# One 512-column product in place of two 256-column ones, with the sum of both halves moved to VectorE

## The chip, the cores and the metric
The kernel runs on one core of one Trainium2 chip. The metric is the device time of one launch in microseconds (us). Three runs of the kernel before gave 2631.38, 2632.57 and 2633.56 us; the median is 2632.57 us.

## The reference, cut to what matters
The reference computes two transformer blocks over 256 tokens (272 with 16 meta tokens in the first), with a model width of 2048, all in float32. Nearly all arithmetic is in dense products of an activation matrix with a weight matrix:

```python
# block 1 (272 tokens; the feed-forward part needs 258, then 256 of them)
proj = rmsnorm(h) @ w_in ; attention of two kinds ; h = h + mix @ w_out
g = x @ w_gate; u = x @ w_up                       # 2048 x 5632 each
h = h + (silu(conv3(g) + conv_b) * u) @ w_down     # 5632 x 2048
# block 2 (256 tokens)
proj = rms_norm(h) @ w_in                          # q, k, v, pool input, gates
m = sigmoid(g0)*(ya @ w_br_a) + sigmoid(g1)*(yb @ w_br_b) + sigmoid(g2)*(yc @ w_br_c)
h = h + m @ w_out
h = h + (silu(h' @ w_gate) * (h' @ w_up)) @ w_down # h' = rms_norm(h)
return rms_norm(h)
```

## The kernel before, in words
**Products.** A float32 product is made of three fp32r products. A weight w is split into its rounded value `whi` and the rest `wlo`, an activation x likewise into `xh` and `xl`, and whi·xh + whi·xl + wlo·xh is added up in PSUM. Weights are the stationary operand, 128x128; the activations (features on partitions, tokens along the free dimension) are the moving one. The moving columns are read alternately from the two halves of the token range (`in_turn`), and who reads PSUM undoes that order (`bank`, `halves`).

**Chunks and groups.** The weights come as a stream of 924 chunks of 128x1024 float32 (512 KB). A chunk holds two row tiles (k) of four output blocks (`ob`) of 128 columns, so that one chunk is 8 pairs of (k tile, block) and 24 matmuls (`chunk`, L1372 to L1374). A group is the run of chunks that fills the four PSUM banks `acc[:, 0..3]`: 8 chunks (CD) for an inner width of 2048, 22 (CF) for 5632, 4 (CH) for 1024. Block `ob` accumulates in bank `ob`, columns 0 to n.

**The pipeline of a chunk.** SyncE loads it to `raw` (a ring of 4 slots). ScalarE (ACT) rounds it to `whi` (`high_part`, L480). VectorE (DVE) subtracts to get `wlo` (`low_part`, L841). TensorE (PE) waits for `lo_ready` at each chunk, and raises `chunk_used` at its end; ACT waits for that of four chunks earlier before it writes a slot. ACT and DVE each run through their instructions in program order and are AHEAD = 2 chunks in front: before they turn to the results of a group, they have made the first two chunks of the next group, and not its third.

**The end of a group.** DVE waits for each block (`wait_block`) and takes it out of PSUM, one 128x256 instruction a block, which raises `bank_free`: times 1/rms into `quad_a`, `quad_b` or `qkvu` (`times_rms`, L861); for the up projection times the activated gate (L1220); for a residual straight into h (L882). PE starts block `ob` of the next group when bank `ob` is free.

**Stages, in order** (chunks): the first block's projections and attention (106, tokens 272 or 258), FFN (11 turns of a gate group of 258 columns and an up group of 256), DOWN (4 groups of 22), IN2 (6 groups), IN2S (8 groups, MOBA attention beside them), MERGEA (4 turns of a gate group and a branch group of 4 chunks, the stick-breaking attention beside them), POOL (2), MERGE (8 turns of gate group and branch group), OUT2 (4 groups), FFN2 (11 turns of gate and up group), DOWN2 (4 groups of 22).

**What follows a group, by stage.** After a gate group of FFN2, ACT applies SiLU (L708), and only then makes `whi` of the up group's third chunk. After an up group (FFN, FFN2), ACT rounds the product to `acth` (L711), DVE subtracts to `actl` (L1224), and only then makes `wlo` of the next group's third chunk. After a gate group of MERGEA and MERGE, ACT applies the sigmoid (L750). After a group of DOWN or OUT2, DVE makes `wlo` of the third chunk, then four parts of `xl` (L891) for which ACT makes `xh` (L502), then waits for ACT's square (L506) and adds it up (L866, L868), and then makes `wlo` of the fourth.

Of the kernel before, what the change touches and what calls it, by code (L numbers as in the profile page):

```python
# [108 lines left out]
def build(nc, hT, wts, vecs, ident, ones, tril, triu, cos_sin, na_bias, relT, onehot,  # L109
# [3 lines left out]
    with ExitStack() as ctx:  # L113
# [8 lines left out]
        xh = sb("xh", [P, DB, L], F32R)  # L122
        xl = sb("xl", [P, DB, L], F32R)
# [74 lines left out]
        acth = at("acth", 0, [P, FFB, SEQ], F32R)  # L198
        actl = at("actl", FFB * SEQ * 4, [P, FFB, SEQ], F32R)

        qkvu = at("qkvu", 0, [P, 56, SEQ])
        yah = at("yah", 57344, [P, HEADS, SEQ], F32R)
        yal = at("yal", 65536, [P, HEADS, SEQ], F32R)
# [14 lines left out]
        ych = at("ych", 24576, [P, HEADS, SEQ], F32R)  # L218
        ycl = at("ycl", 32768, [P, HEADS, SEQ], F32R)
        ybh = at("ybh", 40960, [P, HEADS, SEQ], F32R)  # L220
        ybl = at("ybl", 49152, [P, HEADS, SEQ], F32R)
        msum = at("msum", T0, [P, DB, SEQ])
        mh = at("mh", 0, [P, DB, SEQ], F32R)
        ml = at("ml", T0, [P, DB, SEQ], F32R)
# [12 lines left out]
        bank_free = sem("bank_free")  # L237

# [79 lines left out]
        AT_END = AT_DOWN2.past(4 * CF, 4)  # L318
        assert nc.sbuf_base <= arena
# [31 lines left out]
        def bank(ob, n, rows=slice(0, P)):  # L351

            return acc[rows, ob, 0:n].rearrange("p (a s) -> p s a", s=2)
# [52 lines left out]
        def _(pool):  # L406
# [34 lines left out]
            pool.wait_ge(bank_free, 4 + 4 * AT_MERGEA.g)  # L441
# [31 lines left out]
        def _(act):  # L473
# [19 lines left out]
            def residual(at, b0, gain, cols, dst_cols, chunks, first=0, ahead=False):  # L493

                high_parts(at, chunks, first)
                if ahead:
                    high_part(shifted(at, chunks, 1), 0)
                for ob in range(4):

                    act.wait_ge(bank_free, groups_behind(at, 4, 4 + ob + 1))  # L500
# [202 lines left out]
            def ffn(start, turn0, k, before_silu):  # L703
                def turn(at, i, first):
# [5 lines left out]
                    act.wait_ge(bank_free, groups_behind(at, 4, 4 + 8))  # L710
# [6 lines left out]
            ffn(AT_FFN, 0, 4, 3)  # L717
            high_part(AT_DOWN, 0)
            with act.Fori(0, 2) as i:
                for k in range(2):  # L720
                    residual(shifted(Turn(AT_DOWN, i, 2 * CF, 2), k * CF, k), i * 8 + 4 * k, "mix2_g", slice(META, L),
                             slice(0, SEQ), CF, 1, True)
# [6 lines left out]
            act.wait_ge(bank_free, 4 + 4 * AT_IN2S.g)  # L729
# [18 lines left out]
            def gate(at):  # L748
                act.wait_ge(bank_free, groups_behind(at, 4, 4 + 4))
# [7 lines left out]
            with act.Fori(0, 4) as i:  # L757
                at = Turn(AT_MERGEA, i, CD + CH, 2)
                for j in range(CD + CH):
# [22 lines left out]
                    if j == CD - 1:  # L782
                        gate(at)
# [18 lines left out]
            for i in range(4):  # L802
                for b in range(2):
                    at = AT_MERGE.past((2 * i + b) * (CD + CH), 2 * (2 * i + b))
                    high_parts(at, CD, 1 - b)
                    gate(at)
# [4 lines left out]
            with act.Fori(0, 4) as i:  # L811
                residual(Turn(AT_OUT2, i, CD, 1), i * 4, "ffn2_g", slice(META, L), slice(0, SEQ), CD, 1, True)
            act.preload_act_table_set(LN_EXP)
            ffn(AT_FFN2, 11, 6, 0)
# [5 lines left out]
            for k in range(3):  # L820
                residual(AT_DOWN2.past(k * CF, k), 4 * k, None, slice(META, L), None, CF, min(k, 1), True)
# [15 lines left out]
        def _(dve):  # L837
# [25 lines left out]

            def add_squares(n):
# [5 lines left out]
            def residual(at, b0, chunks, gain, cols, dst_cols, xh0, sq0, scale=None, first=0, ahead=False):  # L870
# [3 lines left out]
                for ob in range(4):  # L874
                    wait_block(at, chunks, ob)
                    src = bank(ob, n)
                    if scale is not None:
                        dve.tensor_tensor(halves(quad_a[:, ob, 0:n]), src, halves(scale[:, 0:n]), ALU.mult)
                        dve.drain()
                        src = halves(quad_a[:, ob, 0:n])  # L880
                    hb = halves(flat(h[:, bass.ds(b0 + ob, 1), cols]))
                    dve.tensor_tensor(hb, src, hb, ALU.add).then_inc(bank_free, 1)  # L882
# [299 lines left out]
            def ffn(start, turn0, k, conv):  # L1182
# [3 lines left out]
                def turn(at, i, done=0):  # L1186
                    low_parts(at, CD, done)
                    dve.wait_ge(rs_ready, k)
                    times_rms(at, CD, lambda ob: (quad_a if conv else quad_b)[:, ob, 0:nt], slice(c0, L))
# [28 lines left out]
                    for ob in range(4):  # L1218
# [21 lines left out]
            times_rms(AT_IN2, CD, lambda ob: qkvu[:, ob, :], slice(META, L))  # L1240
            dve.memset(ss[:], 0.0)
            with dve.Fori(1, 6) as i:
                at = Turn(AT_IN2, i, CD, 1)
                low_parts(at, CD)
                times_rms(at, CD, lambda ob: flat(qkvu[:, bass.ds(i * 4 + ob, 1), :]), slice(META, L))
            with dve.Fori(0, HEADS) as i:
# [12 lines left out]
                times_rms(at, CD, lambda ob: flat(qkvu[:, bass.ds(i * 4 + (3 * HEADS + ob), 1), :]), slice(META, L))  # L1259

            def gates(at):
                times_rms(at, CD, lambda ob: quad_a[:, ob, 0:SEQ], slice(META, L))

            def branch(at, i, gate_n, dst):

                dve.wait_ge(gate_out, gate_n)
                for ob in range(4):
                    wait_block(at, CH, ob)
                    dve.tensor_tensor(halves(dst(ob)), bank(ob, SEQ), halves(quad_a[:, ob, 0:SEQ]), ALU.mult).then_inc(bank_free, 1)
# [8 lines left out]
            with dve.Fori(0, 4) as i:  # L1278
                start = Turn(AT_MERGEA, i, CD + CH, 2)
                for j in range(CD + CH):  # L1280
# [3 lines left out]
                    if j == CD + CH - 1:  # L1284
                        masked_exponentials(hd)
                        branch(shifted(start, CD, 1), i, i + 1, lambda ob: flat(msum[:, bass.ds(i * 4 + ob, 1), :]))
# [35 lines left out]
            with dve.Fori(0, 4) as i:  # L1322
                for b in range(2):
# [5 lines left out]
                    branch(at, i, i * 2 + (5 + b), lambda ob: quad_b[:, ob, 0:SEQ])  # L1329
# [24 lines left out]
        def _(pe):  # L1354
            def chunk(at, j, chunks, x_hi, x_lo, n, blocks=4, width=P, row=GC, per_chunk=2, halfway=None):
# [491 lines left out]
```

## Time and profile before

| | |
|---|---|
| median of three runs | 2632.57 us |
| profiled execution | 2633.74 us, its span 2632.1 us |
| PE, PEld busy | 2608.5 us, 2578.4 us (22,866 instructions each) |
| DVE, ACT, POOL busy | 1658.2, 1252.0, 85.8 us |
| granted TensorE clock | 0.999 of full speed |
| DMA | 497.83 MB, mean 189 GB/s |

PE is the matmul pipe and PEld its weight loads. Matmuls overlap each other, so that the durations of one line add up to more than the span; the pace of PE is read from the starts in the timeline. "Idle before" is the time that an engine stood still just before an instruction, with the work that released it.

### The profile page before, as it was taken

To read this page: it belongs to the slowest core of one execution; us is meant where nothing else is said; L and a number is where in the kernel's file an instruction comes from. 1 tells how busy PE (TensorE), PEld (TensorE's weight loads), DVE (VectorE), ACT (ScalarE), POOL (GpSimd) and SP (SyncE) were. 2 spreads that over 40 slices of the span, in tenths; PEclk is the share of its full clock that TensorE was granted. 3 is DMA by queue.
4 is the path that set the end of the run, shared out by engine and by line. 5 is a ranking of instruction groups with operands and counts; after the bars stand their busy time and mean duration, and the time that the engine had idled before them with its cause. 6 is when DMAs were issued, how large, how long until landed. Compare 5 with 4: busy or idle time off the path is not lost.

```text
span 2632.1 us, 58075 instructions
## 1 busy us (share of the span) xinstructions
PE 2608.5 (99%) x22866; PEld 2578.4 (98%) x22866; DVE 1658.2 (63%) x2223; ACT 1252.0 (48%) x1563; POOL 85.8 (3%) x123
## 2 busy tenths in 40 slices
PE   9999999999999999999999999999999999999998
PEld 8999999999999999999999999999999999999998
DVE  7778786666666555555556776656665555655554
ACT  6456654434444444434445564444554444444443
POOL 0000000000000000000111500000000000000000
PEclk9999999999999999999999999999999999999999
DMA  7543446555565566666555455556555555566655
GB/s 251 156 140 120 150 168 200 192 199 199 183 209 185 205 190 207 199 193 193 190 191 174 160 183 195 200 196 199 194 198 194 197 194 191 191 193 207 199 192 185
DMA packets 138876, 497.83 MB, mean 189 GB/s; under 512 B 16544, under 2 KB 17056, under 8 KB 138752
## 3 DMA queue, kind: packets, MB, share of 16 engines
q1 hardware_dynamic: 135728, 491.34, 56.0%
q0 software_dynamic: 3024, 4.66, 0.9%
q8 instruction: 99, 1.62, 0.2%
q14 instruction: 25, 0.20, 0.0%
HBM read 493.31 MB, written 2.62 MB: 188 GB/s over the span
## 4 chain that ended last, share of the span: by engine, by line
PE 92%; DVE 4%; ACT 2%; DMA 1%; issue 1%; DVEq 1%; SPq 0%; ACTq 0%
PE acc L1372 30%; PE acc L1373 29%; PE acc L1374 29%; DVE wlo L841 1%; PE aux L1425 1%; DMA h<-in_hT 1%; ACT whi L480 1%; PE aux L1405 0%; PE aux L1503 0%; DMA raw<-in_wts 0%; DVEq L914 0%; PE aux L1416 0%; PE aux L1506 0%; PE aux L1619 0%; DVE qn_na L987 0%
## 5 line engine op out<-in xcount | busy, mean ns | idle before, releaser
L841 DVE TENSOR_TENSOR wlo<-raw,whi 128x1024 fp32r<-128x1024 f32 x926 | 1120.6, 1228 | 706.7 <-ACT whi L480 703.2
L1372 PE MATMUL acc<-xh,whi 128*128 128x256 f32 (+3 forms) x4968 | 1377.2, 277 | 4.3 <-DVE wlo L841 2.0
L1374 PE MATMUL acc<-xh,wlo 128*128 128x256 f32 (+3 forms) x4968 | 1367.4, 275 | 0.0
L1373 PE MATMUL acc<-xl,whi 128*128 128x256 f32 (+3 forms) x4968 | 1367.4, 275 | 0.0
L480 ACT ACTIVATE whi<-raw 128x1024 fp32r<-128x1024 f32 x926 | 958.9, 1054 | 791.6 <-PE acc L1374 774.3
L1372 PEld LDWEIGHTS acc<-xh,whi 128*128 128x128 f32 (+1 forms) x4968 | 951.0, 191 | 11.0 <-issue 5.9
L1373 PEld LDWEIGHTS acc<-xl,whi 128*128 128x128 f32 (+1 forms) x4968 | 951.2, 191 | 0.4
L1374 PEld LDWEIGHTS acc<-xh,wlo 128*128 128x128 f32 (+1 forms) x4968 | 951.2, 191 | 0.0
L1372 PE MATMUL acc<-acth,whi 128*128 128x256 f32 x1408 | 387.3, 275 | 0.0
L1373 PE MATMUL acc<-actl,whi 128*128 128x256 f32 x1408 | 387.2, 275 | 0.0
L1374 PE MATMUL acc<-acth,wlo 128*128 128x256 f32 x1408 | 387.2, 275 | 0.0
L1372 PEld LDWEIGHTS acc<-acth,whi 128*128 128x128 f32 x1408 | 270.3, 192 | 0.2 <-DVE wlo L841 0.2
L1374 PEld LDWEIGHTS acc<-acth,wlo 128*128 128x128 f32 x1408 | 270.3, 192 | 0.0
L1373 PEld LDWEIGHTS acc<-actl,whi 128*128 128x128 f32 x1408 | 270.3, 192 | 0.0
L861 DVE TENSOR_TENSOR quads<-acc,rstd 128x256 f32<-128x256 f32 (+1 forms) x136 | 57.9, 425 | 53.6 <-PE acc L1374 53.1
L708 ACT ACTIVATE quads<-quads 128x1024 f32<-128x1024 f32 x22 | 23.3, 1059 | 108.6 <-DVE quads L1206 57.9
L711 ACT ACTIVATE acth<-quads 128x1024 f32 (+1 forms) x22 | 23.3, 1060 | 106.5 <-DVE quads L1220 106.5
L1372 PE MATMUL acc<-mh,whi 128*128 128x256 f32 x256 | 70.4, 275 | 0.0
L1373 PE MATMUL acc<-ml,whi 128*128 128x256 f32 x256 | 70.4, 275 | 0.0
L1374 PE MATMUL acc<-mh,wlo 128*128 128x256 f32 x256 | 70.4, 275 | 0.0
L434 POOL DMA_DIRECT2D bias<-distances x64 | 32.7, 513 | 1022.8 <-PE acc L1374 780.7
L1372 PEld LDWEIGHTS acc<-mh,whi 128*128 128x128 f32 x256 | 49.2, 192 | 0.0
(303 smaller groups left out, 2259.5 us busy)
## 6 DMA issues: line engine op xcount, KB each, us to landing
raw<-in_wts SPq DMA_DIRECT2D x928, 512.0 KB, 4.2
bias<-distances POOLq DMA_DIRECT2D x64, 32.0 KB, 3.5
bias<-in_na_bias POOLq DMA_DIRECT2D x8, 217.7 KB, 3.4
h<-in_hT SPq DMA_DIRECT2D x3, 544.0 KB, 5.1
out_T<-result SPq DMA_DIRECT2D x3, 384.0 KB, 2.8
h<-in_hT SPq DMA_DIRECT2D x2, 272.0 KB, 4.1
distances<-quads POOLq DMA_DIRECT2D x1, 512.0 KB, 12.5
out_T<-result SPq DMA_DIRECT2D x1, 512.0 KB, 2.7
```

Source lines behind the costliest of these rows:

```text
L434: pool.dma_start(bias2[p:p + COPIES, t, :], bass.AP(dist_dram.tensor, i * (DISTS + 1) + (SEQ - 1 - t * P - p), [[HEADS * (DISTS + 1) - 1, ...
L480: act.activation(whi[:, slot_of(at, j), :], raw[:, slot_of(at, j), :], ACT.Copy).then_inc(hi_ready, 1)
L708: act.activation(quad_b[:, :, 0:SEQ], quad_b[:, :, 0:SEQ], ACT.Silu).then_inc(silu_out, 1)
L711: act.activation(acth[:, bass.ds(i * 4, 4), :], quad_a[:, :, 0:SEQ], ACT.Copy).then_inc(act_hi, 1)
L841: dve.tensor_tensor(wlo[:, slot_of(at, j), :], raw[:, slot_of(at, j), :], whi[:, slot_of(at, j), :].bitcast(F32), ALU.subtract).then_inc(l ...
L861: dve.tensor_tensor(halves(dst(ob)), bank(ob, n), halves(scale[:, cols]), ALU.mult)\
L1372: pe.matmul(dst, hi, x_hi(kt), start=kt == 0, stop=False)
L1373: pe.matmul(dst, hi, x_lo(kt), start=False, stop=False)
L1374: last = pe.matmul(dst, lo, x_hi(kt), start=False, stop=kt == chunks * per_chunk - 1)
L1425: last = pe.matmul(aux[:, 3, q:a.nq], a.vt[0:nk, kt, :], a.pt[0:nk, kt, q:a.nq], start=kt == 0, stop=kt == len(a.kt) - 1)
```

## The change
In every group with 256 tokens, but for the branch products (`yah`, `ybh`, `ych`) and the pooling products, the three products of a pair become two: whi times [xh | xl], 512 columns, into both halves of the bank, and wlo times xh, 256 columns, into the first half. Groups of 272 or 258 tokens keep three products. The high and low parts of an activation move into one tile (`xs`, `acts`, `ms`, ...) so that one access pattern reads both. What PSUM then holds in two halves is added by DVE: `sum_parts` reduces 512 columns to 256 a block, and the factor (1/rms, the activated gate) or the residual is applied by one 128x1024 instruction behind it. Those who waited for the fourth `bank_free` of such a group now wait for `group_out`, raised by that last instruction. The last stage's residual (DOWN2) adds the two halves to h one after the other, a 128x256 instruction each.

```diff
-        xh = sb("xh", [P, DB, L], F32R)
-        xl = sb("xl", [P, DB, L], F32R)
+        xs = sb("xs", [P, 2, DB, L], F32R)
+        xh, xl = xs[:, 0], xs[:, 1]
...
+        def both_parts(ob):
+
+            return acc[:, ob, 0:2 * SEQ].rearrange("p (k a s) -> p s a k", k=2, s=2)
...
+            def sum_parts(at, chunks, dst):
+
+                for ob in range(4):
+                    wait_block(at, chunks, ob)
+                    dve.tensor_reduce(halves(flat(dst[:, ob:ob + 1, :])), both_parts(ob), AX_X, ALU.add)\
+                        .then_inc(bank_free, 1)
+                dve.drain()
+
+            def sums_times_rms(at, chunks, dst):
+
+                sum_parts(at, chunks, dst)
+                dve.tensor_tensor(dst, dst, rstd[:, META:L].unsqueeze(1).to_broadcast([P, 4, SEQ]), ALU.mult)\
+                    .then_inc(group_out, 1)
...
+                elif sq0 is not None:
+                    sum_parts(at, chunks, quad_a[:, :, 0:SEQ])
+                    hq = h[:, bass.ds(b0, 4), cols]
+                    dve.tensor_tensor(hq, hq, quad_a[:, :, 0:SEQ], ALU.add).then_inc(group_out, 1)
+                else:
+                    for ob in range(4):
+                        wait_block(at, chunks, ob)
+                        hb = halves(h[:, b0 + ob, cols])
+                        dve.tensor_tensor(hb, bank(ob, SEQ), hb, ALU.add)
+                        dve.drain()
+                        dve.tensor_tensor(hb, bank(ob, SEQ, first=SEQ), hb, ALU.add).then_inc(bank_free, 1)
...
-                    for ob in range(4):
-                        wait_block(at, CD, ob)
-                        dve.tensor_tensor(halves(quad_a[:, ob, 0:SEQ]), bank(ob, SEQ), halves(quad_b[:, ob, 0:SEQ]),
-                                          ALU.mult)\
-                            .then_inc(bank_free, 1)
+                    product = quad_a[:, :, 0:SEQ]
+                    sum_parts(at, CD, product)
+                    dve.tensor_tensor(product, product, quad_b[:, :, 0:SEQ], ALU.mult).then_inc(group_out, 1)
...
-                    act.wait_ge(bank_free, groups_behind(at, 4, 4 + 8))
+                    act.wait_ge(group_out, wide(i))
...
+            def wide_chunk(at, j, chunks, x, x_hi, halfway=None):
...
+                        def low():
+                            return pe.matmul(acc[:, ob, 0:SEQ], wlo[:, slot, c:c + P], x_hi(kt), start=False, stop=False)
+
+                        def high(first, final):
+                            return pe.matmul(acc[:, ob, 0:2 * SEQ], whi[:, slot, c:c + P], x(kt), start=first, stop=final)
+
+                        if kt < 2 * chunks - 1:
+                            high(kt == 0, False)
+                            last = low()
+                        else:
+                            low()
+                            last = high(False, True)
...
+            def both(t, first=0):
+                cols = slice(first, first + SEQ)
+                return (lambda kt: t[:, :, kt, cols].rearrange("p k (s a) -> p k a s", s=2),
+                        lambda kt: in_turn(t[:, 0, kt, cols]))
```

## Rows read from the trace of the kernel before
**Rows 1.** The page: busy time, share of the span, instructions.
```profile
PE 2608.5 (99%) x22866; PEld 2578.4 (98%) x22866; DVE 1658.2 (63%) x2223; ACT 1252.0 (48%) x1563; POOL 85.8 (3%) x123
```
**Rows 2.** Waits of PE: us in total, times, longest.
```profile
PE acc L1372 <- DVE wlo L841: 2.7, 5, 0.8
```
**Rows 3.** Groups by form, PE: count, busy us, mean ns, idle before.
```profile
L1372 PE MATMUL acc<-xh,whi 128*128 128x256 f32 x3776 | 1042.4, 276 | 1.2 <-DVE wlo L841 1.2
```
**Rows 4.** Timeline of PE, 256 columns, first and 30th: start, duration.
```profile
799.73 0.28 PE L1374 MATMUL acc<-xh,wlo 128*128 128x256 f32 x1
...
802.97 0.28 PE L1373 MATMUL acc<-xl,whi 128*128 128x256 f32 x1
```
**Rows 5.** Timeline of PE: 258 columns (first, 13th) and 272 (first, 15th).
```profile
300.16 0.28 PE L1374 MATMUL acc<-mixbh,wlo 128*128 128x258 f32 x1
...
301.50 0.28 PE L1374 MATMUL acc<-mixbh,wlo 128*128 128x258 f32 x1
...
149.87 0.28 PE L1374 MATMUL acc<-xh,wlo 128*128 128x272 f32 x1
...
151.49 0.28 PE L1373 MATMUL acc<-xl,whi 128*128 128x272 f32 x1
```
**Rows 6.** Timeline of PEld where PE stood still: DOWN2's third chunk.
```profile
2390.08 0.19 PEld L1372 LDWEIGHTS acc<-acth,whi 128*128 128x128 f32 x1 [0.17 <-DVE wlo L841]
2390.18 0.19 PEld L1373 LDWEIGHTS acc<-actl,whi 128*128 128x128 f32 x1
```
**Rows 7.** Timeline of PE: a 384-column fp32r matmul and the next.
```profile
1557.96 0.34 PE L1635 MATMUL aux<-sbsh,tril_r 128*128 128x384 f32 x1
1558.14 0.33 PE L1635 MATMUL aux<-sbsl,tril_r 128*128 128x384 f32 x1
```
**Rows 8.** Groups by form, DVE: takes from PSUM, a reduction, a 128x1024 factor.
```profile
L861 DVE TENSOR_TENSOR quads<-acc,rstd 128x256 f32<-128x256 f32 x92 | 39.1, 425 | 35.1 <-PE acc L1374 34.6
L1215 DVE TENSOR_TENSOR quads<-quads,rstd 128x1024 f32<-128x1024 f32 x22 | 26.8, 1219 | 0.0
L904 DVE TENSOR_REDUCE small<-aux 86x3 f32<-86x816 f32 x8 | 8.0, 1003 | 6.1 <-PE aux L1506 6.1
```
**Rows 9.** Timeline of DVE in FFN2: gate group's end, up group's end.
```profile
2063.17 0.42 DVE L861 TENSOR_TENSOR quads<-acc,rstd 128x256 f32<-128x256 f32 x1 [0.25 <-PE acc L1374]
2065.72 3.50 DVE L841 TENSOR_TENSOR wlo<-raw,whi 128x1024 fp32r<-128x1024 f32 x3 [2.12 <-ACT whi L480]
...
2084.61 0.42 DVE L1220 TENSOR_TENSOR quads<-acc,quads 128x256 f32<-128x256 f32 x1 [0.25 <-PE acc L1374]
2087.54 4.75 DVE L841 TENSOR_TENSOR wlo<-raw,whi 128x1024 fp32r<-128x1024 f32 x4
```
**Rows 10.** Timeline of PE: first matmul of third, third, fourth (DOWN), MERGEA chunk.
```profile
2068.33 0.28 PE L1372 MATMUL acc<-xh,whi 128*128 128x256 f32 x1
...
2089.77 0.28 PE L1372 MATMUL acc<-xh,whi 128*128 128x256 f32 x1
...
927.14 0.28 PE L1372 MATMUL acc<-acth,whi 128*128 128x256 f32 x1
...
1441.79 0.38 PE L1372 MATMUL acc<-yah,whi 128*128 128x256 f32 x1 [0.32 <-DVE wlo L841]
```
**Rows 11.** Timeline of DVE at a group's end in DOWN.
```profile
919.43 0.42 DVE L882 TENSOR_TENSOR h<-acc,h 128x256 f32 x1 [0.24 <-PE acc L1374]
...
922.49 1.19 DVE L866 TENSOR_TENSOR quads<-quads 128x512 f32<-128x512 f32 x2
...
924.10 3.49 DVE L841 TENSOR_TENSOR wlo<-raw,whi 128x1024 fp32r<-128x1024 f32 x3
```
**Rows 12.** Timeline of ACT there: the last xh, the square.
```profile
920.11 0.51 ACT L502 ACTIVATE xh<-h,vec  x1 [0.16 <-issue]
920.52 1.04 ACT L506 ACTIVATE quads<-h 128x1024 f32 x1
```

More of the change, by code:

```diff
@@ L491, in inv_rms, with residual @@
                 act.activation(dst, dst, ACT.Exp, scale=-0.5).then_inc(done, 1)
-            def residual(at, b0, gain, cols, dst_cols, chunks, first=0, ahead=False):
+            def residual(at, b0, gain, cols, dst_cols, chunks, first=0, ahead=False, wide=None):
                 high_parts(at, chunks, first)
@@ L497, in residual @@
                     high_part(shifted(at, chunks, 1), 0)
+                if wide is not None:
+                    act.wait_ge(group_out, wide)
                 for ob in range(4):
-                    act.wait_ge(bank_free, groups_behind(at, 4, 4 + ob + 1))
+                    if wide is None:
+                        act.wait_ge(bank_free, groups_behind(at, 4, 4 + ob + 1))
                     if gain is not None:
@@ L782, in _ @@
                     if j == CD - 1:
-                        gate(at)
+                        gate(i + (WIDE_MERGEA + 1))
                     if j in (1, CD):
@@ L1354, in _ @@
         def _(pe):
+            def wide_chunk(at, j, chunks, x, x_hi, halfway=None):
+                slot = slot_of(at, j)
+                pe.wait_ge(lo_ready, chunks_behind(at, j + 1))
+                for ob in range(4):
+                    if halfway and ob == 2:
+                        halfway()
+                    if j == 0:
+                        pe.wait_ge(bank_free, groups_behind(at, 4, ob + 1))
+                    for t in range(2):
+                        c = t * GC + ob * P
+                        kt = 2 * j + t
+                        def low():
[5 more added lines that the diff above has]
+                            last = low()
+                        else:
+                            low()
+                            last = high(False, True)
+                    if j == chunks - 1 and ob < 3:
+                        last.then_inc(block_done, 1)
+                last.then_inc(chunk_used, 1)
             def chunk(at, j, chunks, x_hi, x_lo, n, blocks=4, width=P, row=GC, per_chunk=2, halfway=None):
@@ L1383, in group @@
                         pe.wait_ge(*waits[j])
-                    chunk(at, j, chunks, *args, **kwargs)
+                    (wide_chunk if len(args) == 2 else chunk)(at, j, chunks, *args, **kwargs)
             def token_sums(wait, n_wait, of=ss):
@@ L1395, in norm_in_first_group @@
                         pe.wait_ge(x_ready, x0 + j // 2 + 1)
-                    chunk(at, j, CD, x_hi, x_lo, n)
+                    (wide_chunk if len(xs) == 2 else chunk)(at, j, CD, *xs)
                     if j == CD - 3:
@@ L1590, in turn @@
                 def turn(at, first):
-                    xs = (lambda kt: in_turn(xh[:, kt, c0:c0 + n]), lambda kt: in_turn(xl[:, kt, c0:c0 + n]), n)
-                    norm_in_first_group(at, *xs, x0) if first else group(at, CD, *xs)
-                    group(shifted(at, CD, 1), CD, lambda kt: in_turn(xh[:, kt, c1:c1 + SEQ]),
-                          lambda kt: in_turn(xl[:, kt, c1:c1 + SEQ]), SEQ)
+                    gate = both(xs, c0) if n == SEQ else (
+                        lambda kt: in_turn(xh[:, kt, c0:c0 + n]), lambda kt: in_turn(xl[:, kt, c0:c0 + n]), n)
+                    norm_in_first_group(at, gate, x0) if first else group(at, CD, *gate)
+                    group(shifted(at, CD, 1), CD, *both(xs, c1))
                 turn(start, True)
@@ L1601, in down @@
                 for k in range(4):
-                    group(start.past(k * CF, k), CF, x1(acth), x1(actl), SEQ,
+                    group(start.past(k * CF, k), CF, *both(acts),
                           waits={0: (act_ready, a0 + 10), CF - 2: (act_ready, a0 + 11)} if k == 0 else {})
@@ L1607, in _ @@
             down(AT_DOWN, 0)
-            norm_in_first_group(AT_IN2, x2(xh), x2(xl), SEQ, 12)
+            norm_in_first_group(AT_IN2, both(xs), 12)
             with pe.Fori(1, 6) as i:
-                group(Turn(AT_IN2, i, CD, 1), CD, x2(xh), x2(xl), SEQ)
+                group(Turn(AT_IN2, i, CD, 1), CD, *both(xs))
             with pe.Fori(0, HEADS) as i:
@@ L1613, in _ @@
                 for j in range(CD):
-                    chunk(at, j, CD, x2(xh), x2(xl), SEQ)
+                    wide_chunk(at, j, CD, *both(xs))
                     if j == 0:
@@ L1640, in _ @@
                     if j < CD:
-                        chunk(start, j, CD, x2(xh), x2(xl), SEQ)
+                        wide_chunk(start, j, CD, *both(xs))
                     else:
```

98 lines of the change are left out of this document (54 added, 44 removed).

## The prediction
> **What bounds the kernel now.** I read the busy line of the page first, then the waits of PE, then PE's timeline, and last the timelines of DVE and ACT around the ends of groups. PE and its weight loads are busy for 99% and 98% of the span, DVE for 63%, ACT for 48% [rows 1]: the reader is to see that only PE can bound the whole. PE hardly ever waits for the weights' low parts, 2.7 us in all [rows 2]. So the pace of the matmuls sets the time: 30 starts in a row lie 3.24 us apart, 111.7 ns a matmul of 256 columns [rows 4], which is 2.68 us a chunk of 24.
>
> What sets this pace? Matmuls of 258 columns have the same 111.7 ns, those of 272 have 115.7 [rows 5]. At 2.4 GHz 272 columns take 113.3 ns, which leaves 2.4 ns a matmul; by that 256 would take 109.1. It takes 111.7 whether it has 256 or 258 columns, so something that does not depend on them is longer. The weight load fits: where PE had stood still, the next load started 0.10 to 0.11 us after the first [rows 6]. Granted clock is full throughout (0.999).
>
> **The matmuls.** The wide stages are 680 chunks (FFN's up groups 88, DOWN 88, IN2 48, IN2S 64, MERGEA 32, MERGE 64, OUT2 32, FFN2 176, DOWN2 88) with 8 pairs each, 5440 pairs; the largest part of them is in one row [rows 3], whose operand feeds IN2, IN2S, MERGEA, MERGE and both up and gate products. A pair costs 3 x 111.7 = 335.0 ns now. After the change its 512 columns take 213.3 + 2.4 = 215.7 ns, and the load of wlo hides behind them. The 256 columns behind them keep 111.7 ns, because the load for the next whi still has to fit behind them. The pair is 327.4 ns, 7.6 ns less; a chunk 0.06 us less. MERGEA is bound by its attention chain (a chunk there starts on the arrival of wlo, the last line of [rows 10]), so I give it nothing. The other 648 chunks give 648 x 8 x 7.55 = 39 us.
>
> The trace has no 512-column fp32r matmul. From below: with no weight wait on the short one, the pair is 768 columns and two overheads, 325 ns, and the gain 52 us. From above: the widest fp32r matmul, 384 columns read straight, is followed after 0.18 us [rows 7], 18 ns over 160 + 2.4; with that on each wide matmul the pair would be 345 ns and the stages 57 us slower than now. I take 327.4, by the 272 row, because that one is read in the same alternating order as the new operand, which the 384 one is not.
>
> The Trainium skill, "TensorE: Matmul & The Clock Gate", section Back-to-back issue gap, gives columns/2.4 plus about 2.5 ns, so 215.8 ns for 512; the 272 columns agree. Its section on LDWEIGHTS gives columns/1.2, 106.7 ns for 128, which agrees with the load that followed a wait. By both pages' figures the pair would be 327 to 328 ns as well.
>
> **What DVE has to do at a group's end.** Now a block is taken out in 0.425 us, and the last one starts as its block ends [rows 8, 9]. New is a reduction of 512 columns. The reduction row is 816 elements in 1.003 us, one element a cycle of 0.96 GHz (0.85) and 0.15 fixed [rows 8]; so 0.533 + 0.15 = 0.69 us. Four of them keep step with PE, whose blocks end 0.655 us apart, since the fixed part overlaps the next. Behind the fourth come a drain, 0.1 to 0.2 us (an estimate: releases of one engine by another take 0.07 to 0.26 in [rows 9, 11, 12]), and one 128x1024 instruction, 1.22 us [rows 8]. The result is late by 0.69 - 0.425 + 0.16 + 1.22 = 1.65 us. From below this could be 1.5; from above, if a reduction over pairs ran at two cycles a column (1.22 us each), the four would fall behind PE's 0.655 and end 2.2 us later than now, which makes it 3.6.
>
> That lateness costs nothing by DVE's load (it is 63% busy). It costs where the third or fourth chunk of the next group depends on it, because ACT and DVE are only two chunks ahead. So the spare time at each kind of handoff has to be held against 1.65 us, and PE also comes earlier by 0.06 us a chunk. A wait that starts adds 0.14 us over the lateness, the visible load and release [rows 6].
>
> *FFN2, gate to up.* DVE ends the gate at 2063.59, then SiLU, then whi, then wlo from 2065.72 to 2066.95; PE takes that chunk at 2068.33 [rows 9, 10]: 1.38 spare. Wait: 1.65 + 0.12 - 1.38 + 0.14 = 0.53 us, 11 times, 5.8 us.
>
> *Up to the next gate.* wlo runs from 2087.54 to 2088.77 behind acth and actl, PE takes it at 2089.77 [rows 9, 10]: 1.00 spare. 1.69 (the first reduction starts late) + 0.12 - 1.00 + 0.14 = 0.95, 10 times, 9.5 us. In FFN the order is the same and the gate chunks are not faster: 0.83 x 10 = 8.3 us.
>
> *FFN to DOWN and FFN2 to DOWN2*, once each: the second already waits now [rows 6], so 1.8 us there, and I take 1.2 for the first: 3.0 us.
>
> *DOWN and OUT2.* The h of all four blocks is now ready at once, 1.65 late, and only then ACT starts its four xh. Four at 0.41 apart, as the square follows the last one [rows 12], and the 1.04 us of the square: it ends at 919.43 + 0.69 + 0.16 + 1.22 + 0.26 + 1.64 + 1.04 = 924.44. Squares are added from 924.5 instead of 922.49 [rows 11], 2.0 late. The fourth chunk's wlo ends at 925.33 now and is taken at 927.14 [rows 10, 11]: 1.81 spare. 2.0 + 0.18 - 1.81 + 0.14 = 0.5, six times; the two last groups (DOWN, OUT2) have a table load behind the square and I take 1.2 each: 5.4 us.
>
> *MERGE, gate to branch*: as gate to up, but the branch chunks are not faster: 0.4 x 8 = 3.2 us. *MERGEA*: no spare at its worst chunk, the last line of [rows 10]; part of the 1.65 is covered by a table load there, I take 1.2 x 4 = 4.8 us. IN2 and IN2S have nothing but wlo behind their results, two chunks (5.2 us) away: nothing. If that cover failed it would be 14 groups of 1 us. DOWN2's last block has one more 128x256 instruction, 0.5 us, at the very end.
>
> Costs: 5.8 + 9.5 + 8.3 + 3.0 + 5.4 + 3.2 + 4.8 + 0.5 = 40.5 us.
>
> **Sum.** 2633.74 - 39.2 + 40.5 = 2635.0 for the profiled execution, which is 1.2 us over the median of the runs. Forecast: 2633.8 us, no difference that can be measured. (0.2%, 5.3 us, is about what can be told from none.) It is a difference of two terms of 40 us each, so that 15% on either moves it out of that bound.
>
> The Trainium skill, "VectorE: DVE Perf Modes", section on the perf-mode tiers, speaks against the change: a tensor_reduce has the 1x rate only, from any memory. The 816-element row agrees. By it a reduction of 512 takes at least 533 ns, as in the sum.
>
> **Rivals.** (1) *Handoffs or matmuls better than counted: faster.* With no weight wait behind the short matmul the gain is 52 us, 2621; with the waits at half, 2613. For it: each wait above is the small remainder of two numbers of 1 to 2 us, and 0.3 us less lateness takes away a third. Against: 256 and 258 columns share one pace [rows 4, 5]. 2602 to 2625.
> (2) *The 512-column matmul has an overhead beyond its columns: slower.* Its place is every wide pair, its price 5.2 us for each ns over 215.7, and the 39 us are gone at 7.5 ns. At the 384 row's 18 ns: 2634 + 5184 x 0.018 = 2727. For it: rows 7. Against: 272 columns in alternating order show nothing of it.
> (3) *The reduction takes two cycles a column: slower.* Then the result is 3.6 us late instead of 1.65. Some 55 handoffs of the list add 1.95 each, 107 us: 2741. Decides from about 0.05 us a reduction, above which four no longer keep step. Against: the one row of a reduction.
> (4) *The change does not reach the pace*: were the load of whi repeated for each half of 512, two loads and 3 x 111.7 would stay and only the handoffs be added, 2673. I count it with (2).
>
> **Chances.** The forecast's case 0.54, with a range of its own of 2620 to 2650, within which 0.13 is faster, 0.26 the same, 0.15 slower; (1) 0.25; (2) and (4) 0.12; (3) 0.09. Faster 0.38, same 0.26, slower 0.36. The range 2604 to 2680 leaves out the high prices of (2) and (3) and the best of (1).
>
> **What would show it.** PE timeline in DOWN: starts 216 and 112 ns apart in turn, chunks of 2.62 us; anything else breaks the first term. PE's waits for wlo go from 2.7 us to some 35 to 40, on the third chunk of FFN and FFN2 groups (0.5 and 0.9 us) and the fourth of DOWN (0.5). The reduction's row reads 0.69 us. FFN and FFN2 get slower by some 4 us each, DOWN, IN2 and IN2S faster by some 2 to 4 each. I am wrong if the wide matmul is not 216 ns, if the reduction is over 0.75, or if DVE's 128x1024 step turns out to overlap what I have it delay.

## The result and the profile after

The kernel after takes 2636.97 us, the median of 14 runs (2636.35 to 2639.57). The kernel before, run beside it, takes 2631.86 us (14 runs, 2631.38 to 2633.56). The ratio is 1.0021 [1.0013, 1.0029]: 5.1 us slower. That is just inside what I had called no change (0.2%, 5.3 us), but the interval leaves 1 out: with 14 runs of each kernel a small loss can be told from none. The profiled execution of after took 2636.78 us, its span 2635.0 us, at a granted clock of 0.999.

The first line is the page's busy line of after, the answer to [rows 1]; the others are its rows by group, as in [rows 3, 8]: count, busy us, mean ns, idle before.

```profile
PE 2582.8 (98%) x17426; PEld 2395.3 (91%) x17426; DVE 1804.9 (68%) x2297; ACT 1243.3 (47%) x1563; POOL 85.5 (3%) x123
...
L1418 PE MATMUL acc<-xs,whi 128*128 128x512 f32 x3776 | 1237.0, 384 | 13.4 <-DVE wlo L861 13.4
L1415 PE MATMUL acc<-xs,wlo 128*128 128x256 f32 x3776 | 991.2, 273 | 0.0
...
L888 DVE TENSOR_REDUCE quads<-acc 128x256 f32<-128x512 f32 x224 | 144.8, 688 | 32.2 <-PE acc L1418 29.4
```

5440 matmuls and their weight loads are gone. PE is busy for less time and stands still for more. DVE has 147 us more to do; the reduction takes 0.688 us.

The next lines are PE's timeline in DOWN (start, duration), which answers to [rows 4]. Two matmuls follow each other 0.22 and 0.11 us apart in turn. Five pairs, from 928.73 to 930.37, take 1.64 us: 0.328 us a pair instead of 0.335.

```profile
928.73 0.27 PE L1415 MATMUL acc<-acts,wlo 128*128 128x256 f32 x1
928.84 0.38 PE L1418 MATMUL acc<-acts,whi 128*128 128x512 f32 x1
929.06 0.27 PE L1415 MATMUL acc<-acts,wlo 128*128 128x256 f32 x1
...
930.37 0.27 PE L1415 MATMUL acc<-acts,wlo 128*128 128x256 f32 x1
```

Against that stand PE's waits (us in total, times, longest), 31.4 us for low parts of weights where [rows 2] had 2.7:

```profile
PE acc L1418 <- DVE wlo L861: 18.0, 33, 1.8
PE acc L1447 <- DVE wlo L861: 13.4, 17, 1.2
```

How such a wait comes about is seen at the end of an up group of FFN2, in the timeline of DVE (start, duration, in brackets what it waited for). It answers to the second half of [rows 9]:

```profile
2041.14 2.48 DVE L888 TENSOR_REDUCE quads<-acc 128x256 f32<-128x512 f32 x4 [0.15 <-issue]
2043.71 1.23 DVE L1266 TENSOR_TENSOR quads<-quads 128x1024 f32<-128x1024 f32 x1
2046.39 1.23 DVE L1268 TENSOR_TENSOR acts<-quads,acts 128x1024 f32 x1 [1.45 <-ACT acts L729]
2047.53 4.62 DVE L861 TENSOR_TENSOR wlo<-raw,whi 128x1024 fp32r<-128x1024 f32 x4
```

The four reductions keep step with PE, the product follows only behind the last of them, and ACT's rounding, DVE's `actl` and the third chunk's wlo are all strung behind it. That wlo is the first of the four in the last line, ready at 2048.75. PE's timeline shows that it had run out of weights by then, and its first matmul starts on that release:

```profile
2047.71 0.27 PE L1415 MATMUL acc<-xs,wlo 128*128 128x256 f32 x1
2048.80 0.48 PE L1418 MATMUL acc<-xs,whi 128*128 128x512 f32 x1 [0.82 <-DVE wlo L861]
2049.12 0.27 PE L1415 MATMUL acc<-xs,wlo 128*128 128x256 f32 x1
```

In DOWN (timeline of DVE, answering to [rows 11]) the sum of h waits for all four blocks, and the square is added up to 931.2 before the fourth chunk's wlo can begin. The last line is PE's, the first matmul of that fourth chunk:

```profile
922.49 2.65 DVE L888 TENSOR_REDUCE quads<-acc 128x256 f32<-128x512 f32 x4 [0.96 <-PE acc L1418]
925.37 1.23 DVE L918 TENSOR_TENSOR h<-h,quads 128x1024 f32 x1 [0.23 <-issue]
926.52 1.22 DVE L861 TENSOR_TENSOR wlo<-raw,whi 128x1024 fp32r<-128x1024 f32 x1
927.65 1.89 DVE L934 SCALAR_TENSOR_TENSOR xs<-h,vec,xs  x4
929.57 1.19 DVE L900 TENSOR_TENSOR quads<-quads 128x512 f32<-128x512 f32 x2
930.84 0.43 DVE L902 TENSOR_TENSOR ss<-ss,quads 128x256 f32<-128x256 f32 x1
931.18 4.62 DVE L861 TENSOR_TENSOR wlo<-raw,whi 128x1024 fp32r<-128x1024 f32 x4
...
932.46 0.48 PE L1418 MATMUL acc<-acts,whi 128*128 128x512 f32 x1 [0.18 <-DVE wlo L861]
```

By stage, each counted from its first matmul to that of the next stage (us, from the starts in the traces, one profiled execution of each; DOWN2 to the end of its last matmul; the columns on the right are experiments told below):

```
stage    before   after  no_sum  third_up  third_first   best
FFN       473.0   479.6   467.7     467.9        468.0  468.4
DOWN      235.8   233.7   230.6     232.3        230.8  230.8
IN2       129.1   127.4   126.2     127.4        126.2  126.2
IN2S      186.4   183.4   182.6     183.7        183.7  183.7
MERGEA    151.7   154.7   150.9     154.7        156.1  154.7
MERGE     257.3   255.9   253.5     255.9        253.5  251.5
OUT2       85.8    85.3    83.8      85.3         83.8   83.8
FFN2      472.1   478.7   461.6     468.0        461.6  461.6
DOWN2     236.3   232.8   231.1     231.3        231.3  231.3
```

The stages with a handoff every 8 chunks and a long chain behind it (FFN, FFN2) lost 6.6 us each, MERGEA 3.0; the others won 12.1 together. That leaves 4.1 us, and 0.6 at the end of the kernel. The two profiled executions differ by only 2.9 us in span, because the first projections, which the change does not alter, took 2.4 us more in that of before, where their first matmul came 0.6 us sooner. Over 14 runs each such differences are gone.

### The profile page after: what moved, and what is told of

It reads as the page before. It is cut to its first block, busy times and chain, and to the rows that moved or that the text cites. A ratio compares the mean times of both kernels' runs of the same rounds, so it can differ in the third digit from the quotient of the medians.

```text
span 2635.0 us, 47348 instructions
## 1 busy us (share of the span) xinstructions
PE 2582.8 (98%) x17426; PEld 2395.3 (91%) x17426; DVE 1804.9 (68%) x2297; ACT 1243.3 (47%) x1563; POOL 85.5 (3%) x123
## 3 DMA queue, kind: packets, MB, share of 16 engines
HBM read 493.31 MB, written 2.62 MB: 188 GB/s over the span
## 4 chain that ended last, share of the span: by engine, by line
PE 77%; DVE 11%; ACT 4%; DVEq 4%; issue 3%; DMA 1%; ACTq 0%; SPq 0%
PE acc L1418 36%; PE acc L1415 18%; PE acc L1447 7%; PE acc L1449 6%; PE acc L1448 6%; DVE wlo L861 3%; DVE quads L888 2%; ACT whi L495 2%; DVEq L1263 1%; DVE quads L1266 1%; DMA raw<-in_wts 1%; ACT acts L729 1%; PE aux L1500 1%; DVEq L890 1%; PE aux L1480 0%
## 5 line engine op out<-in xcount | busy, mean ns | idle before, releaser
L1418 PE MATMUL acc<-xs,whi 128*128 128x512 f32 x3776 | 1237.0, 384 | 13.4 <-DVE wlo L861 13.4
L1415 PE MATMUL acc<-xs,wlo 128*128 128x256 f32 x3776 | 991.2, 273 | 0.0
L1418 PEld LDWEIGHTS acc<-xs,whi 128*128 128x128 f32 x3776 | 698.0, 189 | 106.4 <-DVE wlo L861 20.5
L1415 PEld LDWEIGHTS acc<-xs,wlo 128*128 128x128 f32 x3776 | 723.5, 192 | 12.0
L1418 PE MATMUL acc<-acts,whi 128*128 128x512 f32 x1408 | 460.4, 382 | 3.9 <-DVE wlo L861 3.9
L1415 PE MATMUL acc<-acts,wlo 128*128 128x256 f32 x1408 | 378.6, 273 | 0.0
L1447 PE MATMUL acc<-xs,whi 128*128 128x258 f32 (+1 forms) x1192 | 335.8, 282 | 11.9 <-DVE wlo L861 9.6
L1448 PE MATMUL acc<-xs,whi 128*128 128x258 f32 (+1 forms) x1192 | 329.0, 276 | 0.0
L1449 PE MATMUL acc<-xs,wlo 128*128 128x258 f32 (+1 forms) x1192 | 329.0, 276 | 0.0
L1418 PEld LDWEIGHTS acc<-acts,whi 128*128 128x128 f32 x1408 | 263.9, 189 | 40.7 <-DVE wlo L861 5.4
L1415 PEld LDWEIGHTS acc<-acts,wlo 128*128 128x128 f32 x1408 | 270.1, 192 | 1.7
L1447 PEld LDWEIGHTS acc<-xs,whi 128*128 128x128 f32 x1192 | 226.1, 190 | 20.1 <-DVE wlo L861 11.4
L1448 PEld LDWEIGHTS acc<-xs,whi 128*128 128x128 f32 x1192 | 226.2, 190 | 0.6
L1449 PEld LDWEIGHTS acc<-xs,wlo 128*128 128x128 f32 x1192 | 226.2, 190 | 0.0
```

The lines of the kernel that those rows point to most:

```text
L1415: return pe.matmul(acc[:, ob, 0:SEQ], wlo[:, slot, c:c + P], x_hi(kt), start=False, stop=False)
L1418: return pe.matmul(acc[:, ob, 0:2 * SEQ], whi[:, slot, c:c + P], x(kt), start=first, stop=final)
L1447: pe.matmul(dst, hi, x_hi(kt), start=kt == 0, stop=False)
L1448: pe.matmul(dst, hi, x_lo(kt), start=False, stop=False)
L1449: last = pe.matmul(dst, lo, x_hi(kt), start=False, stop=kt == chunks * per_chunk - 1)
```

## The experiments

My theory had two terms: the pace of the matmuls gives 39 us, and the result that is ready later takes 40 at the handoffs. The rivals put the loss elsewhere: in the wide matmul itself, or in a change that hardly reaches the pace. The first four runs separate the terms and take the pace apart, the last four go for the handoffs.

**no_sum: the matmuls alone.** PE's program of after, but the programs of ACT, DVE and POOL of before. The second half of each bank (whi times xl) is left out of the result. One of the places, against after:

```diff
-                sums_times_rms(at, CD, qkvu[:, bass.ds(i * 4, 4), :])
+                times_rms(at, CD, lambda ob: flat(qkvu[:, bass.ds(i * 4 + ob, 1), :]), slice(META, L))
```

> The changed kernel's wide matmuls with the VectorE, ScalarE and GpSimd programs of the kernel before: the second half of each bank (whi times xl) is left out of the sum, one 128x256 instruction takes out a block, and nothing is multiplied or added afterwards. Theory (two terms that cancel: matmul pace against late results): only the first term is left, 648 chunks x 0.06 us = 39 us and some more in MERGEA, so 2592 to 2595 us, PE waits for wlo back at some 3 us. Rival (the wide matmul itself costs time at the group's ends, or the waits come from less slack by the faster PE): the waits stay and it is 2610 us or more.

Measured: 2593.34 us (2592.27 to 2594.36), 0.9855 [0.9838, 0.9871]. PE's waits for the low parts are as small as in [rows 2]:

```profile
PE acc L1417 <- DVE wlo L856: 1.5, 3, 0.7
...
PE acc L1388 <- DVE wlo L856: 1.2, 2, 0.8
```

So the new matmuls are worth 38.5 us against the kernel before (2631.87 us, run beside it), and all that DVE does for them costs 2636.97 - 2593.34 = 43.6 us. Both terms are there, each about 40 us.

**three_products: the other side of it.** DVE, ACT and the layout of after, but the matmuls back to three of 256 columns (except at the first and last k tile of a group, which start and end the accumulation over the whole bank):

```diff
+                            if first or final:
                                 return pe.matmul(acc[:, ob, 0:2 * SEQ], whi[:, slot, c:c + P], x(kt), start=first, stop=final)
+                            pe.matmul(acc[:, ob, 0:SEQ], whi[:, slot, c:c + P], x(kt)[:, 0], start=False, stop=False)
+                            return pe.matmul(acc[:, ob, SEQ:2 * SEQ], whi[:, slot, c:c + P], x(kt)[:, 1], start=False, stop=False)
```

> The changed kernel's VectorE and ScalarE programs, but whi times [xh | xl] as two matmuls of 256 columns into the two halves (the first and the last k tile of a group keep the 512 one). Theory: the matmul gain goes but for these two k tiles of 16 or 44 (about 4 us of 39 stay), the late results stay: PE waits on the third and fourth chunks, each shorter by 0.12 to 0.18 us as PE comes later, in all about 32 us over the kernel before: 2660 to 2666 us. Rival (the waits are caused by the faster PE): 2632 to 2640 us.

Measured: 2665.96 us (2665.11 to 2668.63), 1.0132 [1.0116, 1.0149]. Its busy line, and then PE's waits:

```profile
PE 2618.9 (98%) x22298; PEld 2563.1 (96%) x22298; DVE 1806.7 (68%) x2297; ACT 1244.2 (47%) x1563; POOL 85.6 (3%) x123
```

```profile
PE acc L1420 <- DVE wlo L861: 11.9, 17, 1.6
PE acc L1450 <- DVE wlo L861: 11.2, 17, 0.9
```

4872 pairs (22298 - 17426) went back to three matmuls, at 7.55 ns each 36.8 us. The waits fell from 31.4 to 23.1 us; a slower PE asks for its weights later. 36.8 - 8.3 = 28.5, and the kernel is 29.0 us slower than after. The two terms are not independent: about a fifth of what PE gains it gives back by arriving sooner where weights are late.

**low_224: what sets the short slot.** The wlo product takes only 224 of its 256 columns (the last 32 are left out):

```diff
-                            return pe.matmul(acc[:, ob, 0:SEQ], wlo[:, slot, c:c + P], x_hi(kt), start=False, stop=False)
+                            return pe.matmul(acc[:, ob, 0:224], wlo[:, slot, c:c + P], x_hi(kt)[:, 0:112, :], start=False, stop=False)
```

> The changed kernel with the wlo product cut to 224 of 256 columns (32 columns of it are left out of the sum). Theory (the short matmul's slot is set by the load of the next whi, 111.7 ns, not by its columns): nothing changes, 2634 to 2639 us, the short slot stays 112 ns. Rival (columns set it): the slot falls to 96 ns, 680 x 8 x 13 ns = 70 us less PE time, some of it given to waits: 2570 to 2590 us.

Measured: 2639.28 us (2637.94 to 2641.88), 1.0029 [1.0016, 1.0042]: not faster than after, with 13 ns less of columns in every pair. It is even 2.3 us slower, 0.3 us beyond the range that I had given; by the stages that lies in FFN (1.1 us) and in DOWN2 with the end (1.7 us), and I did not take it apart. So the columns do not set the short slot. PE's timeline in DOWN, and then the wide matmul's row by group:

```profile
929.84 0.40 PE L1418 MATMUL acc<-acts,whi 128*128 128x512 f32 x1
930.07 0.26 PE L1415 MATMUL acc<-acts,wlo 128*128 128x224 f32 x1
930.16 0.40 PE L1418 MATMUL acc<-acts,whi 128*128 128x512 f32 x1
...
930.82 0.40 PE L1418 MATMUL acc<-acts,whi 128*128 128x512 f32 x1
```

```profile
L1418 PE MATMUL acc<-xs,whi 128*128 128x512 f32 x3776 | 1240.0, 395 | 13.7 <-DVE wlo L861 13.6
```

Three pairs take 0.98 us, 0.327 each, as the theory had it. But I had expected the short slot itself to stay at 0.112 us, and that was wrong: it reads 0.09 to 0.10, and the wide one 0.23 instead of 0.22. To the nanosecond, the medians of the starts in DOWN are 96 and 232 ns here, and 109 and 218 in after, where the forecast had 112 and 216. That fits a start that is recorded when the columns before it are through (by the 272-column row, 2.4 ns over their time: 95.7 ns for 224, 109.1 for 256), with the wait for the weights inside the next matmul's own recorded duration (395 ns instead of 384). Only the sum over a pair can be read from such starts.

That it is the weight load that fills the slot, and not a fixed time that every matmul takes, is shown only in part: no run changes the size of the load. Against a fixed time stands a place in the trace of before, where nine transposes with at most 91 columns to load and 86 to move, and the matmul behind them, start within 0.65 us, 0.07 us each (PE's timeline):

```profile
99.36 0.87 PE L1405 MATMUL aux<-ident_s,sx 86*91 86x86 f32 x9
100.01 0.36 PE L1372 MATMUL acc<-xh,whi 128*128 128x258 f32 x1
```

**straight: the order of the moving columns.** The columns of the wide matmuls and of their 256-column partners are read one after the other instead of in turn from the two halves. DVE's reads of PSUM follow that order (not in this cut); its reduction takes 690 ns instead of 688:

```diff
-                return (lambda kt: t[:, :, kt, cols].rearrange("p k (s a) -> p k a s", s=2),
-                        lambda kt: in_turn(t[:, 0, kt, cols]))
+                return (lambda kt: t[:, :, kt, cols], lambda kt: t[:, 0, kt, cols])
```

> The changed kernel with the moving columns of the wide matmuls and of their 256-column partners read straight instead of alternately from the two halves of the tokens; VectorE reads PSUM in that order; same result. Theory (the 18 ns over its columns that the 384-column fp32r matmul had in the trace of before belong to straight reading): the 512 slot grows from 216 to 235 ns or more and the 256 one to 115 to 120, 5184 pairs x 20 to 27 ns = 100 to 140 us: 2740 to 2780 us. Rival (the 18 ns belonged to that place, or to 384 columns): 2637 us.

Measured: 2739.59 us (2737.92 to 2741.34), 1.0411 [1.0394, 1.0429], just under the range that I had given. PE's timeline in DOWN, and then its waits:

```profile
929.84 0.28 PE L1415 MATMUL acc<-acts,wlo 128*128 128x256 f32 x1
929.96 0.39 PE L1418 MATMUL acc<-acts,whi 128*128 128x512 f32 x1
930.19 0.28 PE L1415 MATMUL acc<-acts,wlo 128*128 128x256 f32 x1
...
930.89 0.28 PE L1415 MATMUL acc<-acts,wlo 128*128 128x256 f32 x1
```

```profile
PE acc L1447 <- DVE wlo L861: 9.3, 17, 0.8
PE acc L1418 <- DVE wlo L861: 6.6, 15, 1.3
```

Three pairs take 1.05 us, 0.350 each, 22.6 ns more than in turn. On the 5184 pairs outside MERGEA that is 117 us, less 15.5 us of waits that fell away: 101.7, and 102.6 were measured. So the order of reading has a price of this size, and the 18 ns of the 384-column matmul in [rows 7] fit it, as I had argued against rival (2) (no run reads that one in turn). The price that I put on that rival (2727) is near what the change would have cost without the alternating order.

**third_up: take the third chunk out of the chain.** In FFN and FFN2, whi and wlo of the third chunk are made before the up group's product instead of behind it; ACT makes that whi before it waits for the group, and DVE the wlo between the reductions and their drain:

```diff
+                    high_part(shifted(at, 2 * CD, 2), 0)
                     act.wait_ge(group_out, wide(i))
...
-            def sum_parts(at, chunks, dst):
+            def sum_parts(at, chunks, dst, third=None):
...
+                if third is not None:
+                    low_part(*third)
                 dve.drain()
```

> The changed kernel, but at the end of an up group (FFN and FFN2) ScalarE makes whi of the next group's third chunk before it waits for the product, and VectorE makes its wlo between the four reductions and the 128x1024 product. Same work, same result. Theory (the time lost is the third chunk's wlo queued behind the late result): the waits of 1.19 us (10 in FFN) and 1.08 us (10 in FFN2) go, and the two of the first DOWN and DOWN2 groups, 24 to 25 us: 2611 to 2614 us. Rival (the wait only moves on to the fourth chunk or to the banks): less than half of it comes back, 2625 us or more.

Measured: 2612.49 us (2612.07 to 2612.68), 0.9924 [0.991, 0.9937]. DVE's timeline at the end of an up group of FFN2:

```profile
2026.60 2.48 DVE L888 TENSOR_REDUCE quads<-acc 128x256 f32<-128x512 f32 x4 [0.15 <-issue]
2029.00 1.22 DVE L861 TENSOR_TENSOR wlo<-raw,whi 128x1024 fp32r<-128x1024 f32 x1
2030.31 1.23 DVE L1268 TENSOR_TENSOR quads<-quads 128x1024 f32<-128x1024 f32 x1
2032.99 1.23 DVE L1270 TENSOR_TENSOR acts<-quads,acts 128x1024 f32 x1 [1.45 <-ACT acts L730]
```

The product itself is now even later, by the 1.2 us of the wlo, and it does no harm: DOWN needs it only after the last turn. FFN loses 11.7 us against after, FFN2 10.7, 22.4 of the 24.5 in all; the rest is in DOWN and DOWN2. The wait was the order of the work and not DVE's load, which is the same (1803.3 us busy against 1804.9). What is left of FFN2 (6.4 us above no_sum) is the gate-to-up handoff (11 times 0.47) and OUT2's last group (1.2).

This run also settles a rival that I had not named. In after ACT waits far longer for the DMA transfers of weights than it did before, 192.7 us in 116 waits against 16.6 in 16, and one could take late transfers for the loss. In third_up ACT still waits 189.3 us for them, and 24.5 us are won all the same.

**third_first: the same at every handoff.** Behind gate groups too, and two chunks ahead of the parts of h in DOWN, IN2 and OUT2:

```diff
-                if ahead:
-                    low_part(shifted(at, chunks, 1), 0)
+                for j in range(int(ahead)):
+                    low_part(shifted(at, chunks, 1), j)
...
-                    sums_times_rms(at, CD, quad_a[:, :, 0:SEQ])
+                    sums_times_rms(at, CD, quad_a[:, :, 0:SEQ], third)
```

> The same order at every handoff: up to gate, gate to up in FFN2, gate to branch in MERGE and MERGEA, and for DOWN and OUT2 both the third and the fourth chunk before ScalarE and VectorE turn to xh, xl and the squares. Theory: nearly all waits that the changed kernel added go (about 38 us by the starts of its chunks), 2598 to 2604 us, within 10 us of the kernel that leaves the sums out (2593). MERGEA keeps its own chain. Rival (waits move on): 2610 us or more.

Measured: 2600.57 us (2600.32 to 2602.23), 0.9878 [0.9863, 0.9894]. FFN2, MERGE, OUT2 and IN2 are back at no_sum's time to 0.1 us (table). MERGEA got 1.4 us slower: there the third chunk's wlo stands in front of a chain of attention steps that is late already.

**branch_wide: the exception of the change.** third_first, with the branch products made wide as well:

```diff
-                        chunk(shifted(start, CD, 1), j - CD, CH, x1(yah), x1(yal), SEQ,
+                        wide_chunk(shifted(start, CD, 1), j - CD, CH, *both(yas),
...
-                for b, (yh, yl) in enumerate(((ybh, ybl), (ych, ycl))):
+                for b, ys in enumerate((ybs, ycs)):
```

> As third_first, and the branch products too as one product of 512 columns and one of 256, their sums by four reductions and one 128x1024 product with the gate. 48 chunks x 0.06 us = 2.9 us less in the matmuls. In MERGE the later result hides (third chunk has 2.1 us to spare in the changed kernel), so 1.9 us come; in MERGEA four longer ends of VectorE's work lie in the chain that bounds it, 1.65 us each, up to 6.6 us. Theory: same as third_first to 5 us slower. Rival (the exception costs time): 2 to 3 us faster.

Measured: 2606.4 us (2605.42 to 2607.36), 0.9901 [0.9886, 0.9916]; 5.8 us slower than third_first, 0.8 more than the 5 that I had allowed. MERGE is 1.9 us faster than in third_first (251.5 us, 32 chunks at 0.06), MERGEA 3.1 slower (159.2) and the two pooling chunks behind it 3.9 slower (10.2 against 6.3), which I had not reckoned with: PE now waits there for a bank that DVE frees late (L1367, the second line):

```profile
PE acc L1423 <- DVE wlo L864: 11.3, 13, 1.8
PE acc L1758 <- DVE ybs L1367: 2.9, 1, 2.9
```

The exception of the change is right in MERGEA and wrong in MERGE.

**best: what the runs point to.** third_first, with MERGEA's order as in after and wide branch products in MERGE only:

```diff
-                        gates(start, (start, j))
+                        gates(start, None)
...
-                    branch(at, i, i * 2 + (5 + b), quad_b[:, :, 0:SEQ])
+                    wide_branch(at, i * 2 + (5 + b), quad_b[:, :, 0:SEQ])
```

> As third_first, but MERGEA keeps the changed kernel's order (by the starts of its chunks third_first made MERGEA 156.1 us from 154.7), and the branch products are wide in MERGE alone (251.5 from 253.5 us in branch_wide, where MERGEA lost 3.1). By these: 2600.6 - 1.4 - 2.0 = 2597 us. Rival (MERGEA's 1.4 us is not due to its order): 2598.5 us, as third_first.

Measured: 2596.91 us (2596.11 to 2597.94), 0.9866 [0.985, 0.9882] against before, 40 us below after. Its waits for low parts:

```profile
PE acc L1459 <- DVE wlo L864: 4.5, 7, 0.8
PE acc L1430 <- DVE wlo L864: 1.6, 3, 0.8
```

It beats both kernels, and it is 3.6 us above no_sum, which does not make the sums at all. Of the 43.6 us that the sums cost, the order of the work gave back 38.1; the wide branches in MERGE gave another 1.9. By the stages, what is left lies in MERGEA (3.8 us over no_sum) and IN2S (1.2), the two stages with attention beside them, and in pieces under 1 us.

## Why the prediction was right, and where it was off

The forecast was 2633.8 us for the median and 1.3 us more than before for the profiled execution; it came out at 5.1 us more. The mechanism was right on both sides, the sum 3.9 us too good: the costs were 3.1 us more than the 40.5 of the forecast, the gain 0.7 less than its 39.2. By my own bound of 0.2% it is the case that I called the same and gave 0.26; I had held faster (0.38) and slower (0.36) each for more likely.

*The pace.* Forecast 216 and 112 ns in turn, 2.62 us a chunk, 39.2 us; measured 2.62 us a chunk and 38.5 us (no_sum); the two slots are recorded as 218 and 109 ns, with the same sum. Both assumptions behind it have a run of their own: no overhead on the wide matmul in alternating order (straight has it), and a short slot that its columns do not set (low_224).

*The lateness.* 0.69 us for the reduction was right (0.688), and so was the step with PE. In FFN2, behind an up group, wlo of the third chunk ended 4.34 us after the first matmul of its group before, and ends 6.16 us after it now (medians): 1.82 later, where the forecast had 1.69. PE's earlier arrival, 0.12, comes on top of both.

*The handoffs.* Against no_sum, from the table, with the 0.6 us at the end:

```
stage      forecast cost   measured (after - no_sum)
FFN              8.3            11.9
DOWN             2.7             3.1     (3 x 0.5 and FFN to DOWN)
IN2              1.2             1.2     (DOWN's last group)
IN2S             0               0.9
MERGEA           4.8             3.8
MERGE            3.2             2.5
OUT2             1.5             1.5
FFN2            16.5            17.1     (with OUT2's last group)
DOWN2            1.8             1.7
end              0.5             0.6
sum             40.5            44.3     (43.6 by the medians)
```

*The term that failed is FFN's up to gate*, "0.83 x 10 = 8.3 us". It measured 1.19 each, and ten times 0.36 us is 3.6 of the 3.9 us. I had counted how late the reductions make the result, and let them start where the takes from PSUM start in the kernel before. In FFN they start later. The lines show the same place in the traces of before (first two) and after (last two): ACT's whi of the next group's second chunk, and DVE's first takes from PSUM. The next group's first matmul is at 602.86 before and at 603.21 after.

```profile
597.70 1.06 ACT L480 ACTIVATE whi<-raw 128x1024 fp32r<-128x1024 f32 x1 [1.62 <-PE acc L1374]
601.31 0.84 DVE L1220 TENSOR_TENSOR quads<-acc,quads 128x256 f32<-128x256 f32 x2 [0.15 <-issue]
...
598.48 1.06 ACT L495 ACTIVATE whi<-raw 128x1024 fp32r<-128x1024 f32 x1 [1.87 <-DMA raw<-in_wts]
602.18 2.48 DVE L888 TENSOR_REDUCE quads<-acc 128x256 f32<-128x512 f32 x4 [0.25 <-PE acc L1418]
```

Before, that whi waits for PE to free its slot; after, in nine of the ten handoffs, it waits for the weights themselves, and so it does in no_sum. In the program a slot of `raw` is loaded anew only when wlo of the chunk in it is made. Behind the convolution and SiLU of a gate group those wlo come late and in a burst, a load takes 4.2 us (the median on the page), and PE comes sooner by 0.06 us for each of the up group's 8 chunks. DVE makes that chunk's wlo and the product with 1/rms before it turns to the group's result, so the first reduction starts 1.13 us before the next group's first matmul (median), where the first take started 1.55 us before it. (Its bracket names PE, but PE's signal for the first block is in the trace 1.79 us before that matmul; what came last was DVE's own work.) In FFN2, which has no convolution, no such handoff waits for weights, and the first reduction starts 1.44 us before it. No run changes the ring or the transfers, so this part is read from the traces and the program alone.

No_sum starts as late as that in FFN (1.08 us), but its four takes of 0.42 us catch up, and the last ends where it did before. Reductions, four in 2.48 us with PE's blocks 0.655 us apart, hardly do: the last ends 1.36 us after the group's first matmul in FFN and 1.04 in FFN2. Wlo of the third chunk then ends 6.40 us after it (median; 5.8 to 6.8) instead of 4.34, 2.06 later and not 1.69. That difference is the 0.36.

In FFN2 the same handoff cost 1.08 each instead of 0.95, and gate to up 0.47 instead of 0.53; the errors partly cancel. FFN to DOWN cost 1.65 instead of 1.2, the other three groups of DOWN 1.5 as forecast.

*MERGEA* cost 3.8 instead of 4.8, and it had a gain of 0.8 where I had given none (151.7 to 150.9 in no_sum): net 3.0. *IN2S* cost 0.9 where I had none; what lies beside it is the other attention, and I did not take that apart. *MERGE* cost 0.3 a handoff instead of 0.4.

*The signs to look for.* The starts, the 0.69 us and the faster DOWN, IN2 and IN2S came as forecast. PE's waits were 31.4 us, below the 35 to 40 that I gave: my waits held 0.14 us each for load and release, and I take it that most of this is not in that list (50 waits, 7 us); FFN and FFN2 lost 6.6 us each instead of about 4, FFN by the term above; for FFN2 my own terms (15.3 + 1.2 of cost, 10.6 of gain) already gave 5.9, so that this sign was put down too low.

*The rivals.* (1) needed better handoffs than counted; they were a little worse. In (2) the overhead is real but bound to the order of reading. (3) is out: 688 ns for 512 elements, less the 150 fixed, is 1.05 ns an element, as in the 816-element row, and not twice that. (4) is out by no_sum, where the pace came in full. Two side sums were loose: the upper bound of 57 us counts all 5440 pairs, where 5184 give 54, and (3) counts some 55 handoffs, where the list has 53. Neither touches the forecast. Where each of the two terms was uncertain by some us, the net was bound to be a matter of luck to 2 or 3 us; the forecast was safe only in saying that the two were near each other.

## What to carry to other kernels

When a bound engine is made faster by giving another one more work, the busy share of that other engine says nothing: look, at each handoff, at what the faster engine needs next and at what is queued in front of it. If the spare time is smaller than the new lateness, first move the work that is needed next in front of the result that can wait; here that turned 5 us of loss into 35 us of gain, all but 1.9 us of it by order alone. And count the faster engine's earlier arrival over the whole stretch in which its suppliers do not speed up, transfers into the ring of buffers among them, and not only over the chunks behind the handoff. A lateness that short instructions make good before the handoff stays when each of them takes as long as the engine's own step.

## What the runs showed of the hardware that I had not expected

Reading the moving fp32r columns one after the other costs more than reading them in turn from two halves of the tile: 350 against 327 ns a pair (2739.6 against 2637.0 us). Before, only one row of 384 columns hinted at it. And the recorded start of a matmul need not be when its weights are there: with 32 columns fewer in front of it, the wide matmul started 13 ns sooner (96 instead of 109) and lasted 11 ns longer, at an unchanged pace.
